# Softmax steps with one exponential or one broadcast scaling for four heads, and low parts ahead of modulation pieces in output projection 1

## The reference, cut to what matters

```python
def compressed_attention(q, kc, vc):
    s = jnp.einsum('bshgd,bnhd->bhgsn', q, kc).astype(jnp.float32) * dh ** -0.5
    s = jnp.where(mask, s, -jnp.inf)
    m = jnp.max(s, axis=-1, keepdims=True)
    e = jnp.where(mask, jnp.exp(s - m), 0.0)
    p = e / jnp.where(den > 0, den, 1.0)          # den = sum of e
    o = jnp.einsum('bhgsn,bnhd->bshgd', p.astype(vc.dtype), vc)

o = g[..., 0:1] * o_cmp + g[..., 1:2] * o_sel + g[..., 2:3] * o_win

x = x + g1[:, None, :] * hybrid_mixer(h, w_in[l], w_out[l], rel_bias)   # layer 1, output projection 1
h = modulate(rms_norm(x, norm_ffn[l]), sh2, sc2)
```

## Time and profile before

| | |
|---|---|
| median of three runs | 1664.22 us |
| the profiled execution's own time | 1664.64 us |
| its span | 1662.9 us |
| mean granted TensorE clock | 0.993 of 2.4 GHz |
| busy: TensorE matmul | 1624.9 us (98%) |
| busy: VectorE | 1228.8 us (74%) |
| busy: ScalarE | 907.1 us (55%) |
| busy: GpSimd | 404.1 us (24%) |

### The profile page before, as it was taken

How to read it: one execution, slowest core, us unless ns; L and a number is a source line. 1 busy time by engine, 2 the same in 40 slices (tenths; PEclk the granted TensorE clock), 3 DMA queues, 4 the chain that set the end, 5 groups by cost and what they waited for, 6 DMA issues and landing times.

```text
span 1662.9 us, 31274 instructions
## 1 busy us (share of the span) xinstructions
PE 1624.9 (98%) x10740; PEld 1437.4 (86%) x10740; DVE 1228.8 (74%) x2419; ACT 907.1 (55%) x1743; POOL 404.1 (24%) x163
## 2 busy tenths in 40 slices
PE   6999999999999999999999999999999999899998
PEld 3986899999999999888888888975799998589997
DVE  4479979599718894887787777767798887776665
ACT  3546544455459996555545555348644445664443
POOL 0870038989885556000000000000000000000000
PEclk9999999999999999999999999999999999999999
DMA  9886875555553334788888875640387775155553
GB/s 341 311 220 235 344 217 179 186 179 178 188 178 112 113 111 148 257 298 286 287 294 286 290 276 173 190 178 2 128 302 276 286 246 142 62 168 188 188 189 102
DMA packets 107638, 346.37 MB, mean 208 GB/s; under 512 B 18531, under 2 KB 24451, under 8 KB 107556
## 3 DMA queue, kind: packets, MB, share of 16 engines
q1 hardware_dynamic: 101092, 339.19, 60.6%
q10 hardware_dynamic: 6464, 6.14, 1.2%
HBM read 343.11 MB, written 1.12 MB: 207 GB/s over the span
## 4 chain that ended last, share of the span: by engine, by line
PE 91%; DVE 3%; ACT 3%; issue 1%; DMA 1%; ACTq 1%; DVEq 0%; SPq 0%
PE banks L675 26%; PE banks L676 26%; PE banks L677 26%; PE banks L1023 3%; PE banks L871 2%; PE banks L837 1%; PE banks L889 1%; ACT arena L1369 1%; PE banks L941 1%; PE banks L708 1%; ACT weights_high L1311 1%; PE banks L709 1%; PE banks L712 1%; DVE arena L1756 1%; PE banks L737 0%
## 5 line engine op out<-in xcount | busy, mean ns | idle before, releaser
L1311 ACT ACTIVATE weights_high<-ring 128x1024 fp32r<-128x1024 f32 x470 | 494.6, 1053 | 314.5 <-PE banks L677 303.7
L675 PE MATMUL banks<-ht_high,weights_high 128*128 128x256 f32 x1936 | 556.8, 288 | 3.5 <-DVE ht_low L1834 3.4
L677 PE MATMUL banks<-ht_high,weights_low 128*128 128x256 f32 x1936 | 548.0, 283 | 0.0
L676 PE MATMUL banks<-ht_low,weights_high 128*128 128x256 f32 x1936 | 547.9, 283 | 0.0
L635 POOL TENSOR_TENSOR weights_low<-ring,weights_high 128x1024 fp32r<-128x1024 f32 x158 | 402.8, 2565 | 264.5 <-ACT weights_high L1311 264.1
L1806 DVE TENSOR_TENSOR weights_low<-ring,weights_high 128x1024 fp32r<-128x1024 f32 x312 | 380.4, 1222 | 90.9 <-ACT weights_high L1311 89.6
L675 PEld LDWEIGHTS banks<-ht_high,weights_high 128*128 128x128 f32 x1936 | 371.1, 192 | 7.0 <-issue 4.2
L676 PEld LDWEIGHTS banks<-ht_low,weights_high 128*128 128x128 f32 x1936 | 371.4, 192 | 2.6
L677 PEld LDWEIGHTS banks<-ht_high,weights_low 128*128 128x128 f32 x1936 | 371.1, 192 | 0.0
L1756 DVE SCALAR_TENSOR_TENSOR arena<-arena,cs 128x1024 f32<-128x1024 f32 x80 | 103.4, 1300 | 42.7 <-DMA arena<-in_ada 37.6
L675 PE MATMUL banks<-weights_high,hidden_high 128*128 128x512 f32 x256 | 100.3, 392 | 0.0
(11 more groups left out here) (282 smaller groups left out, 2573.8 us busy)
## 6 DMA issues: line engine op xcount, KB each, us to landing
ring<-in_stream SPq DMA_DIRECT2D x490, 512.0 KB, 3.5
arena<-in_ada SPq DMA_DIRECT2D x88, 512.0 KB, 5.7
ada_ring<-in_ada SPq DMA_DIRECT2D x56, 512.0 KB, 4.2
arena<-gate_store SPq DMA_DIRECT2D x5, 512.0 KB, 6.1
bias_high<-bias_rows ACTq DMA_DIRECT2D x1, 2048.0 KB, 17.6
X<-in_x SPq DMA_DIRECT2D x1, 1024.0 KB, 5.8
bias_low_moba<-bias_rows ACTq DMA_DIRECT2D x1, 1024.0 KB, 8.7
bias_low_dsa<-bias_rows ACTq DMA_DIRECT2D x1, 1024.0 KB, 8.9
```

The lines of the kernel that those rows point to most:

```text
L675: pe.matmul(out, wh, xh, start=start, stop=False, **kw)
L676: pe.matmul(out, wh, xl, start=False, stop=False, **kw)
L677: return pe.matmul(out, wl, xh, start=False, stop=stop, **kw)
L1311: act.activation(WH[:, c % HIGHS, :], ring[:, c % SLOTS, :], ACT.Copy).then_inc(S["high_ready"], 1)
```

## The change

It has three parts.

1. A cmp step no longer gives ScalarE four exponentials with bias and sum. VectorE subtracts the maxima itself (one addition of the negated maximum, broadcast, from PSUM into the buffer `PACKED` in SBUF), ScalarE takes one exponential over the four heads in place, and VectorE takes the sums with one reduction. `PACKED` moves from the probabilities' buffer to one of its own, and the exponential of a cmp step no longer waits for the transposes of two steps before.
2. A step with 128 columns scales its probabilities with one broadcast product over four heads in place of four instructions.
3. In output projection 1 the four low parts stand each ahead of a pair of modulation pieces, not behind it.

```diff
@@ VCC = A(A_VCC, 4, 2, P)
-        PACKED = A(A_P, 2, 4, T)[:, :, 0, 0:P]
+        PACKED = A(A_T1, 2, T)[:, :, 0:P]
@@ def exps(s):
                 act.wait_ge(S["negmax_ready"], n + 1)
+                if s["kind"] == "cmp":
+                    act.activation(four(s), four(s), ACT.Exp).then_inc(S["exp_done"], 1)
+                    return
                 if n >= 2:
                     act.wait_ge(S["probs_transposed"], n - 1)
@@ def maxima(s):
+                if s["kind"] == "cmp":
+                    link(dve.tensor_reduce(negmax[:, n % 2, :], src, AX, ALU.max, negate=True))
+                    dve.tensor_tensor(four(s).rearrange("p (a h) c -> p a h c", a=2), src,
+                                      negmax[:, n % 2, :].rearrange("p (a h) -> p a h", a=2).unsqueeze(3).to_broadcast([P, 2, 2, w]),
+                                      ALU.add).then_inc(S["negmax_ready"], 1)
+                    return
@@ def scale_probs(s):
+                if kind == "cmp":
+                    link(dve.tensor_reduce(sums[:, n % 2, :], four(s), AX, ALU.add))
                 link(dve.reciprocal(r, sums[:, n % 2, :]))
...
                 if kind == "cmp":
-                    four = PACKED[:, n % 2, :].rearrange("p (j c) -> p j c", j=4)[:, :, 0:w]
-                    m = dve.tensor_tensor(four, four, r.unsqueeze(2).to_broadcast([P, 4, w]), ALU.mult)
-                for j in range(0 if kind == "cmp" else 4):
+                    m = dve.tensor_tensor(four(s), four(s), r.unsqueeze(2).to_broadcast([P, 4, w]), ALU.mult)
+                elif w == P:
+                    m = dve.tensor_tensor(PR[:, n % 2, :, 0:w], PR[:, n % 2, :, 0:w], r.unsqueeze(2).to_broadcast([P, 4, w]), ALU.mult)
+                for j in range(4 if w > P else 0):
                     m = dve.tensor_scalar(PR[:, n % 2, j, 0:w], PR[:, n % 2, j, 0:w], rsum[:, n % 2, j:j + 1], None, ALU.mult)
@@ output projection 1
             for k in range(DB):
+                if k % 2 == 0:
+                    low(chunk["out1"] + HIGHS + k // 2)
                 ada_mixer1(DB + k)
-                if k % 2:
-                    low(chunk["out1"] + HIGHS + k // 2)
```

More of the change, by code:

```diff
@@ L439, in two_blocks, with four @@
         att3 = plan(lambda g: ["swa"], 16, 32)
+        def four(s):
+            return PACKED[:, s["n"] % 2, :].rearrange("p (j c) -> p j c", j=4)[:, :, 0:N_CMP]
         def width(s):
@@ L1366, in exps @@
                 for j in range(4):
-                    bank, col = (j // 2, j % 2) if s["kind"] == "cmp" else (j % 2, j // 2)
-                    dst = PACKED[:, n % 2, 32 * j:32 * j + w] if s["kind"] == "cmp" else PR[:, n % 2, j, 0:w]
-                    m = act.activation(dst, banks[:, 2 * (n % 2) + bank, col * T:col * T + w],
+                    m = act.activation(PR[:, n % 2, j, 0:w], banks[:, 2 * (n % 2) + j % 2, (j // 2) * T:(j // 2) * T + w],
                                        ACT.Exp, bias=negmax[:, n % 2, j:j + 1], accum_out=sums[:, n % 2, j:j + 1])
```

## The result

| | before | after |
|---|---|---|
| median of 9 runs each | 1663.72 us (1660.94 to 1665.14) | 1667.77 us (1665.86 to 1670.29) |
| ratio, 95% interval | | 1.0027 [1.0017, 1.0038] |
| own time of the profiled execution | 1664.64 us | 1669.41 us |
| its span, clock | 1662.9 us, 0.993 | 1667.6 us, 0.992 |

The change makes the kernel slower by 0.27%, which is 4.5 us with an interval from 2.8 to 6.3 (the two medians lie 4.05 us apart). The forecast was 1666.5 us, +2.1 by its sum; the result lies in the range and 1.3 us above the point.

What follows compares the result with a forecast made beforehand. The prediction took TensorE, 91% of the chain, to bound the kernel. Its terms 2.8 - 0.54 - 0.18 + 0 gave +2.1 us, 1666.7 on the profiled execution or 1666.3 on the median; it said 1666.5, range 1662.8 to 1669.2.

Steps and rivals of the forecast that it cites:

- the chain of part 3: Output projection 1: VectorE waits for ScalarE's high part, `wq` loads go out later, gates begin later; +2.8 us.
- the clock case: Rival, output projection 1: TensorE's clock falls in the new 3.3 us gap; total +3.0 to +3.7, 1667.9 us; chance 0.25.
- the forecast alone: The main course without rivals: +2.1 us, spanning 1665.0 to 1668.0 us; chance 0.48.
- Part 3, VectorE's wait: Output projection 1: VectorE stands idle 1.9 us from 157.16, until ScalarE's first high part is ready.
- Part 3, the loads: SyncE's queue: first `wq` load out at 163.4, not 160.47; the two landings ScalarE needs come at 171.4 and 174.0.
- the term of the gates: End of output projection 1: gates begin at 176.2, not 173.42; +2.8 us, or +1.9 if the loads catch up.
- Part 3, the clock: Ahead of norm 1's transposes: clock at 1.2 GHz makes eight transposes take 2.0 us, not 1.1; up to 1.6 added, 0.9 likely.
- the two rows: Evidence on the clock: after 3.36 us idle in `att3` it fell; between 166 and 171, TensorE busy 1.80 us, it held.
- Part 2: 128-column steps: one scaling shortens TensorE's waits, -0.54 us in `att2` (0.18 in each of three groups), -0.18 in `att3`.
- Part 1: Cmp steps: ScalarE's saved exponentials become longer waits for TensorE, VectorE's added work is covered; 0 us.
- The two cases with a bound on ScalarE or VectorE in `att2`: Rivals: hanging on ScalarE, -4.7 us, 1659.5, chance 0.06; VectorE becoming the bound, 1668, chance 0.06.
- The case in which VectorE's idle time is hidden: Rival, output projection 1: the new order gives -0.4 to 0, the whole -0.7 to -1.1 us, 1663.5; chance 0.15.

Runs made afterwards that it cites:

- e7: Changed kernel with the first two `wq` loads ahead of `out1`'s last two modulation loads, and 12 fillers before norm 1's transposes; 1665.01 us against 1662.63 before.
- e3: Changed kernel with 16 filler matmuls on TensorE ahead of output projection 1's transposes; 1665.15 us, ratio 1.0018 to the kernel before.
- e1: Kernel before with only the new order of low parts in output projection 1; 1668.27 us against 1662.49.
- e4: Changed kernel with the first two `wq` loads issued ahead of the last two modulation loads of `out1`; 1667.07 us, ratio 1.0020 to the kernel before.
- e10: Changed kernel with output projection 1 ordered pieces 8, 9, low, 10, low, 11, low, low, 12 to 15, no added fillers; ratio 1.0004 to the kernel before.
- e5: Kernel before with only the one broadcast scaling in the 128-column steps; ratio 1.0001.
- e6: Kernel before with only the one exponential over four heads in the cmp steps; ratio 1.0001.
- e8: Changed kernel with pieces 8, 9, low, 10, low, 11, low, low, 12 to 15, `wq`'s second low part behind norm 1's last row sum, 9 fillers; 1661.05 us against 1662.63 before.
- e9: Changed kernel with output projection 1's old order and the second low part of `wq`'s first pair behind norm 1's last row sum; 1660.63 us against 1663.15 before.

## Why the prediction was right, and where its sizes were off

The time lies in the range, and the chain of part 3 (VectorE's wait, the later loads, the later gates) was right. But the course that came is not the one to which I gave 0.48: it is the clock case, to which I gave 0.25, and the forecast's +2.1 is half of what was measured. That 1667.77 stands so near that case's 1667.9 is partly luck, since I counted from 1664.22 and 1664.64 and the nine runs of the kernel before have 1663.72. Nor is it inside the forecast alone, though I gave that a span up to 1668.0: its terms reach from +1.2 to +2.8, so to 1667.4 at most.

**Part 3, VectorE's wait.** Forecast 1.9 us, measured 1.85 (the start of the first low part moved by 2.27 - 0.34 = 1.93). Right, and e7 shows it alone. Its gates are 2.06 us late: the other 0.13 us stand at the end of the queue, where the first small operation now follows a piece and not a low part, and starts 1.26 us behind it and not 1.14.

**Part 3, the loads.** The first `wq` load was forecast at 163.4 and came at 163.5. The second was to be there at 174.0, if it kept the 9.6 us that it took in the kernel before. It took 9.2 us in e3, 9.8 in e1 and 10.5 in the kernel after, and was there at 173.7, 174.2 and 172.97 + 2.0 = 175.0. So the term of the gates, +2.8 with bounds 1.9 and 2.8, was 2.5, 3.05 and 3.8 in three executions of the same order. The mis-sized number is the upper bound: I let the load catch up or keep its time to landing, and not take longer, though the DMA engines were full already (a share of 1.02 and 415 GB/s in the first window of the earlier trace rows).

**Part 3, the clock.** I gave the clock case a chance of 0.25 and a price of 0.9 to 1.6 us. It is the term that fails: the clock fell in every kernel with the new gap and without fillers (after, e1, e4 and e10), after 4.26, 3.52, 2.52 and 4.04 us of idle time, and cost 1.4 us in three of them and 2.5 in the kernel after. I had weighed the two rows as if they were alike. In one, TensorE stood 1.43 and 1.77 us with matmuls between; in the other it stood 3.36 us at a stretch, as here. The second is the nearer row. The price, 0.9 to 1.6 us, had an error of its own: in the kernel after the low level lasted to 185.1, 5.1 us behind the first transposes, while in e10 it ended at about 180, 3 us behind them, so from the start of the transposes to the end of the fillers it is 6.43 us and not 5.35. By the rule of the Trainium skill that I had cited ("TensorE: Matmul & The Clock Gate", section "Part 1: The HAM clock gate"), which makes the lower level the default that only activity lifts, the clock case was the expected one; the four kernels agree.

**Part 2.** Forecast -0.54 and -0.18; e5's trace has -0.46 and -0.18 (the first of the three steps gave 0.08 and not 0.18). The one instruction takes 0.69, as the row of the gates said. **Part 1.** Forecast 0, e6's trace and time say 0: what the exponentials lose, ScalarE waits before its copies. The two cases with a bound on ScalarE or VectorE in `att2` fall with it. The case in which VectorE's idle time is hidden falls with e1.

**The sum.** With e1's gates and the clock's usual price: 3.05 + 1.44 - 0.46 - 0.18 = +3.9 us. With the terms of the kernel after's own trace, 3.79 + 2.53 - 0.64 = +5.7. The ratio says +4.5 (2.8 to 6.3). The forecast's +2.1 is too small by the clock, and by up to 1.0 us for the second load (in e3 that term was 0.3 us too large). The two spans differ by 4.7 us: -2.0 ahead of the stage, +6.3 in it, -0.64, and a rest of 1.0. Two places hold most of it: ahead of `att2` TensorE waits 0.88 us for ScalarE where it waited 0.51 (at 1104.33 in the kernel before), and the stretch behind the last cmp step, where the clock is low in both, takes 5.50 us and not 5.11. What shifts them from one execution to the next I have not shown.

## What to carry to other kernels

Before a wait is removed from the engine that bounds the kernel, look at which engine's string leads to the end of the stage: here TensorE's 3.2 us of waits were worth nothing, since VectorE worked without a gap to the end. Moving an instruction to the front of a queue that never idles cost its whole wait, since its input couldn't be there sooner, and everything that counted on the queue's progress, DMA issues among it, moved along. The new gap of TensorE ahead of the transposes was paid twice, once in time and once in clock. Fillers in it held the clock: 12 in e7 cost nothing, 16 in e3 ran 0.3 us over.

## What the runs showed of the hardware

- The low level of the clock, 1.2 GHz, lasted 3 us behind gaps of 2.52, 3.52 and 4.04 us (e4, e1, e10) and 5 us behind one of 4.26 us (the kernel after), with TensorE busy nearly all that time in each: the last two gaps are nearly the same, and had two prices, 1.4 and 2.5 us.
- At the start of `att2` the clock falls in some executions and not in others: it falls in the kernel before, and in e10 and the kernel after, and not in e8 and e9, which have parts 1 and 2 as those two do. The two windows, first of the kernel before and then of e8, stand at the same place of the program: a granted clock of 0.59 against 1.00, and the way from the first of the 64 products ahead of `att2` (L1179, in e8 L1183) to the last cmp scores takes 2.5 us less in e8 (1094.3 to 1162.8 and 1091.6 to 1157.6), 0.5 of it by part 2. One trace each doesn't tell whether e8's shift in time or chance did this; e9 is as fast there, e10 lies between. A part of what separates single spans is this, and perhaps of e8's and e9's lower times.

```profile
1112.00:1120.00 8.00, 8.00 (x48) 6.26 (x46) 3.88 (x15) 3.10 (x11) 0.00 (x0) 0.59 0.00 1
```

```profile
1109.00:1117.00 8.00, 6.95 (x61) 4.67 (x59) 5.92 (x23) 3.00 (x7) 0.00 (x0) 1.00 0.00 2
```

- 512 columns as one product of two tensors took 0.69 us on VectorE; as four instructions of 128 columns with a scalar for each they took 0.88. With the same columns, one instruction cost less than four.
